# A two-block network on one core: output products of two heads issued together in the second attention, S5 tables computed beside the experts, four norms whose roots use 128 columns, and a row maximum taken in the instruction that adds the bias

## The reference, cut to what matters

```
def first_block(x, c, ...):
    for layer in range(DEPTH):                      # DEPTH = 2
        h = modulate(rmsnorm(x, norm1_w[layer]), shift1, scale1)
        if layer % 2 == 0:
            ...  mix = concat([pool_mixer(u), chunk_attention(q, k, v, rel_bias)]) @ mix_w_out
        else:
            mix = mamba2_mixer(h, ...)
        x = x + gate1 * mix
        h2 = modulate(rmsnorm(x, norm2_w[layer]), shift2, scale2)
        x = x + gate2 * hier_moe(h2, ...)           # 32 experts, top 2 per token
    return rmsnorm(x, final_norm_w)
...
def fox_attention(q, k, v, f_logit, q_gain, k_gain):  # 8 heads of 64, 512 rows
    q, k = rms_norm(q, q_gain), rms_norm(k, k_gain)
    c = cumsum(log_sigmoid(f_logit))
    s = (q @ k.T) * B_HEAD_DIM ** -0.5 + c[query] - c[key]
    s = where(key <= query, s, NEG_INF)
    return softmax(s) @ v
...
def s5_mixer(u, a_re, a_im, log_dt, b_re, b_im, c_re, c_im, d):  # 64 groups, 64 states, 16 channels
    dt = exp(log_dt)
    ab = exp(a * dt)                                # complex, from magnitude, sine and cosine
    bb = (ab - 1) / a * b                           # complex, 64 x 64 x 16
    x_t = ab * x_(t-1) + bb @ u_t                   # scan over 512 rows
    return real(c @ x) + d * u
...
def second_block(x, p, ...):
    for i in range(DEPTH):
        h = rms_norm(x, norm_mix[i])
        if i % 2 == 0:  x = x + concat([gmlp_mixer(u_a, v_a), fox_attention(...)]) @ ev_w_out
        else:           x = x + glu(gelu(s5_mixer(h)))
        x = x + conv_ffn(rms_norm(x, norm_ffn[i]))
        x = x + sigmoid(rms_norm(x) @ ple_w_gate) * (p[i] @ ple_w_proj)
```

## Time and profile before

| | |
|---|---|
| median of 3 runs | 2632.39 us (2631.26 to 2634.85) |
| the profiled execution | 2631.74 us |
| its span in the trace | 2630.0 us |
| mean granted clock of PE | 0.944 of full speed |
| busy share | PE 90%, PEld 69%, DVE 59%, POOL 56%, ACT 27% |
| moved by DMA | 374.40 MB, mean 142 GB/s |

### The profile page before, as it was taken

One profiled execution on the slowest core, in us unless ns is written; L12 is line 12 of the kernel. 1 busy time (PEld: TensorE's weight loads), 2 busy tenths in 40 slices (PEclk: granted clock), 3 DMA queues, 4 the chain that ended last, 5 costly groups with the idle time before them and its releaser, 6 DMA issues.

```text
span 2630.0 us, 33090 instructions
## 1 busy us (share of the span) xinstructions
PE 2366.2 (90%) x12200; PEld 1806.6 (69%) x12200; DVE 1558.4 (59%) x1986; ACT 700.7 (27%) x1170; POOL 1484.7 (56%) x1272
## 2 busy tenths in 40 slices
PE   4988989959999998896798799999987899999998
PEld 2764755537777776553585588888866788888887
DVE  6879832166878765224897666662249926666223
ACT  2113212223434422122223232220025613222011
POOL 4830345455554552553672166667779657666774
PEclk7977989979999997998897999999998999999999
DMA  8845879533323234994331133332330223333231
GB/s 318 255 162 206 293 285 360 190 125 105 102 91 112 93 112 178 393 357 163 84 116 60 49 96 96 96 96 93 114 97 25 57 64 96 96 96 96 88 112 64
DMA packets 316737, 374.40 MB, mean 142 GB/s; under 512 B 52250, under 2 KB 259886, under 8 KB 316502
## 3 DMA queue, kind: packets, MB, share of 16 engines
q1 hardware_dynamic: 253840, 313.82, 35.6%
q0 software_dynamic: 28352, 31.04, 3.6%
q10 hardware_dynamic: 34438, 28.08, 3.5%
HBM read 410.20 MB, written 39.68 MB: 171 GB/s over the span
## 4 chain that ended last, share of the span: by engine, by line
PE 29%; issue 24%; POOL 23%; DVE 11%; DMA 10%; ACT 1%; POOLq 0%; ACTq 0%; SPq 0%; DVEq 0%
POOL WL L853 15%; PE PAIR L545 6%; POOL WH L849 6%; PE PAIR L546 6%; PE PAIR L547 6%; DMA XG<-htok_scratch,GATHER_I 4%; PE BANK L1823 4%; DMA ADA_A<-in_ada_w 2%; PE BANK L2259 1%; PE PAIR L1847 1%; PE PAIR L1809 1%; DVE ADA_SUM L652 1%; DMA PAIR_W<-y_scratch 1%; POOL EXTRA_W L2007 1%; DMA RAW<-in_ffn_w_up 1%
## 5 line engine op out<-in xcount | busy, mean ns | idle before, releaser
L853 POOL TENSOR_TENSOR WL<-RAW,WH 128x512 fp32r<-128x512 f32 x584 | 819.0, 1432 | 12.2
L545 PE MATMUL PAIR<-HH,WH 128*128 128x512 f32 x1792 | 710.0, 396 | 39.4 <-POOL HL L1142 27.2
L546 PE MATMUL PAIR<-HL,WH 128*128 128x512 f32 x1792 | 700.9, 391 | 0.0
L547 PE MATMUL PAIR<-HH,WL 128*128 128x512 f32 x1792 | 700.7, 391 | 0.0
L848 POOL TENSOR_TENSOR TURN<-ONES 128x1 f32<-128x1 f32 x146 | 36.8, 252 | 848.7 <-PE PAIR L547 751.3
L545 PEld LDWEIGHTS PAIR<-HH,WH 128*128 128x128 f32 x1792 | 338.6, 189 | 123.2 <-issue 44.2
L546 PEld LDWEIGHTS PAIR<-HL,WH 128*128 128x128 f32 x1792 | 338.9, 189 | 71.0 <-issue 2.2
L547 PEld LDWEIGHTS PAIR<-HH,WL 128*128 128x128 f32 x1792 | 338.4, 189 | 71.5
L849 POOL TENSOR_SCALAR WH<-RAW 128x2048 fp32r<-128x2048 f32 x146 | 284.7, 1950 | 0.0
L545 PE MATMUL PAIR<-FHH,WH 128*128 128x512 f32 x352 | 138.7, 394 | 0.0
L547 PE MATMUL PAIR<-FHH,WL 128*128 128x512 f32 x352 | 138.0, 392 | 0.0
(11 more groups left out here) (540 smaller groups left out, 4074.7 us busy)
## 6 DMA issues: line engine op xcount, KB each, us to landing
PAIR_W<-in_moe_w SPq DMA_DIRECT2D x96, 1024.0 KB, 9.9
RAW<-in_ffn_w_up SPq DMA_DIRECT2D x88, 512.0 KB, 4.8
ADA_B<-in_ada_w SPq DMA_DIRECT2D x30, 1024.0 KB, 5.3
RAW<-in_ssm_w_in SPq DMA_DIRECT2D x48, 512.0 KB, 4.8
ADA_A<-in_ada_w SPq DMA_DIRECT2D x18, 1024.0 KB, 6.9
RAW<-in_ffn_w_down SPq DMA_DIRECT2D x32, 512.0 KB, 4.2
RAW<-in_ev_w_in SPq DMA_DIRECT2D x20, 512.0 KB, 4.6
RAW<-in_mix_w_in SPq DMA_DIRECT2D x16, 512.0 KB, 6.6
```

Of the source, the lines that this page charges most:

```text
L545: nc.tensor.matmul(o, wh, xh, start=start, stop=False)
L546: nc.tensor.matmul(o, wh, xl, start=False, stop=False)
L547: return nc.tensor.matmul(o, wl, xh, start=False, stop=stop)
L853: ins = pool.tensor_tensor(WL[:, s, c], RAW[:, s, c], WH[:, s, c].bitcast(F32), ALU.subtract)
```

## The change

The diff does five things.

1. **Norms 0, 2, 8 and the final one.** The sums are formed by four products per tile with 32 columns of ones each, so that row block j of 128 stands in partitions 32j to 32j + 31 and only 128 columns are left. Root and reciprocal work on 128 columns. Four products with one column of the identity spread the factor over 128 partitions and 512 columns of a PSUM bank, and DVE multiplies X by that bank. The final norm's weighted sum is made by PE too.
2. **S5 tables.** The vectors, powers, B products, angles and TURN_NEW are computed in MoE 1: DVE does one slice after HID of slots 1 to 10 and 12 to 19, ACT one in slots 0, 2, 8, 11 and 13 to 20. BRAW is loaded in slot 0, and the TURN_NEW saves go out on ACT's queue, not SP's. TAB stays in SBUF, so its save and reload are gone.
3. **Maximum.** In both attentions one instruction adds the bias and takes the row maximum. The factor HD ** -0.5 goes into the copy of Q (att0) or the gain of Q (att1).
4. **Outputs in att1.** The products of two heads are issued after the odd head's transposes and scores, alternating between the two halves of 64 columns.
5. `dve_sum` of the final norm is gone from the residual's loop, and `pool_s5_index` moves ahead into MoE 1.

```diff
+    def pe_sums(bank, at, weights, tile, first, last):
+        for j in range(NT):
+            ins = nc.tensor.matmul(bank[32 * j:32 * j + 32, at:at + P], weights, tile[:, j * P:j * P + P], start=first, stop=last)
+        return ins
...
-            ins = nc.tensor.matmul(bank[:], ONES[:], SQ[:, k % 2, :], start=k == 0, stop=k == KD - 1)
+            ins = pe_sums(bank, 0, ONES[:, 0:32], SQ[:, k % 2, :], k == 0, k == KD - 1)
...
+    def pe_factor(b, at):
+        for j in range(NT):
+            ins = nc.tensor.matmul(BANK[b % 4][:, j * P:j * P + P], IDENT[:, 32 * j:32 * j + 1].broadcast_to([P, P]),
+                                   RSTD[:, at:at + P], start=True, stop=True)
+        ins.then_inc(bank_ready, 1)
...
+        both, one = (take_bank(pe, plan.b[f"norm{FINAL}"] + i) for i in range(2))
+        for k in range(KD):
+            pe.wait(sq_ready)
+            weighted = pe_sums(both, 0, FINAL_SQ[:, k:k + 1].broadcast_to([P, 32]), SQ[:, k % 2, :], k == 0, k == KD - 1)
+            ins = pe_sums(one, 0, ONES[:, 0:32], SQ[:, k % 2, :], k == 0, k == KD - 1)
...
-            if k >= 2:
-                act.wait(part_used)
-            act.e.activation(TMP[:, k % 2, :], X[:, k, :], ACT.Square, scale=norm_gain[FINAL](k)).then_inc(part_ready, 1)
-        act.passed(part_used, 1)
...
-        dve.e.scalar_tensor_tensor(RSTD[:], FINAL_VAR, EPS, RSTD[:], ALU.mult, ALU.add).then_inc(var_ready, 1)
+        both, one = RSTD[:, 0:P], RSTD[:, P:2 * P]
+        dve.link(dve.e.tensor_scalar(both, full_bank(dve, b)[:, 0:P], 1.0 / D, None, ALU.mult))
+        c = b + 1
+        dve.e.tensor_scalar(one, full_bank(dve, c)[:, 0:P], 1.0 / D, EPS, ALU.mult, ALU.add).then_inc(bank_free[c % 4], 1)
+        dve.e.wait_ge(bank_free[c % 4], c // 4 + 1)
+        dve.e.scalar_tensor_tensor(both, one, EPS, both, ALU.mult, ALU.add).then_inc(var_ready, 1)
         dve.wait(root_ready)
-        dve.e.reciprocal(RSTD[:], RSTD[:]).then_inc(bank_free[b % 4], 1)
-        dve.e.wait_ge(bank_free[b % 4], b // 4 + 1)
+        dve.e.reciprocal(both, both).then_inc(bank_free[b % 4], 1)
+        dve.e.reciprocal(one, one).then_inc(total_ready, 1)
...
-            dve.e.scalar_tensor_tensor(norm_buffer(k), X[:, k, :], BOTH_GAIN[:, k:k + 1], RSTD[:], ALU.mult, ALU.mult).then_inc(norm_pre, 1)
+            dve.e.scalar_tensor_tensor(norm_buffer(k), X[:, k, :], BOTH_GAIN[:, k:k + 1], factor[:], ALU.mult, ALU.mult)\
+                 .then_inc(norm_pre if k < KD - 1 else bank_free[b % 4], 1)
...
-                ins = dve.e.scalar_tensor_tensor(HF[:, k, :], X[:, k, :], gain(k), RSTD[:], ALU.mult, ALU.mult)
-                if k in (0, KD - 1):
+                ins = dve.e.scalar_tensor_tensor(HF[:, k, :], X[:, k, :], gain(k), factor[:], ALU.mult, ALU.mult)
...
-        act_copy_pairs(act, "mixin", 2, 2, Q0, False)
+        act_copy_pairs(act, "mixin", 2, 2, Q0, False, scale=HD ** -0.5)
...
+        def outputs(heads):
+            p = p0 + 1
+            pe.e.wait_ge(evac[p % 2], p // 2 + max(0, heads[0] // 2 * 2 - 2))
+            for h in heads:
+                b = att_bank(n, h, 3)
+                pe.e.wait_ge(bank_free[b % 4], b // 4 + 1)
+            o = out_half(n, heads[0] // 2)
             for kt in range(NT):
-                ins = nc.tensor.matmul(o[a:a + HD, kt * P:SEQ], v[:, kt, h * HD:h * HD + HD],
-                                       pt[:, h % 2, TRI_AT[kt]:TRI_AT[kt] + SEQ - kt * P],
-                                       start=kt == 0, stop=kt == NT - 1)
-            ins.then_inc(w["out"], 1)
+                for h in heads:
+                    a = (h % 2) * HD
+                    ins = nc.tensor.matmul(o[a:a + HD, kt * P:SEQ], v[:, kt, h * HD:h * HD + HD],
+                                           pt[:, h % 2, TRI_AT[kt]:TRI_AT[kt] + SEQ - kt * P],
+                                           start=kt == 0, stop=kt == NT - 1)
+            ins.then_inc(w["out"], len(heads))
...
-            outputs(h)
+            if n == 0:
+                outputs((h,))
+            elif h % 2:
+                outputs((h - 1, h))
...
-                    ins = dve.e.scalar_tensor_tensor(s[:, h % 2, SEG[j]:SEG[j] + wide], bank[:, at:at + wide],
-                                                     HD ** -0.5, bias(h)[:, SEQ - wide:SEQ], ALU.mult, ALU.add)
+                    ins = dve.e.tensor_tensor_reduce(s[:, h % 2, SEG[j]:SEG[j] + wide], bank[:, at:at + wide],
+                                                     bias(h)[:, SEQ - wide:SEQ], 1.0, LOWEST, ALU.add, ALU.max,
+                                                     MX[:, h % 2, 0, j:j + 1])
...
-            for j in range(NT):
-                ins = dve.e.tensor_reduce(MX[:, h % 2, 0, j:j + 1], s[:, h % 2, SEG[j]:SEG[j] + P * (j + 1)], AX.X, ALU.max)
-            dve.link(ins)
...
-            elif h:
-                dve_s5_turning(dve, h - 1)
...
-        if n:
-            dve_s5_turning(dve, KD - 1)
...
+                if layer:
+                    act_s5_slice(act, s)
...
+            if layer:
+                dve_s5_slice(dve, s)
...
+            dve_final_gains(dve)
+            for par in range(2):
+                dve.e.wait_ge(turn_saved[par], 8 * KD)
...
-            if layer and i:
-                for k in (2 * i - 2, 2 * i - 1):
-                    dve_sum(dve, k, TMP)
-        if layer:
-            for k in (KD - 2, KD - 1):
-                dve_sum(dve, k, TMP)
...
-    def sp_s5_reload(engine):
-        w, sp = s5_sems, engine.e
-        engine.wait(w["spilled"], 32)
-        engine.wait(half_ready, 4)
-        sp.dma_start(TAB[:].rearrange("p a t n -> p (a t n)"), tab_dram).then_inc(w["tab_back"], 16)
-    def sp_s5_save(engine):
-        w, sp = s5_sems, engine.e
-        for k in range(KD):
-            par = k % 2
-            engine.wait(w["turning"], 2)
-            sp.dma_start(turn_dram[k], TURN_NEW[:, par].rearrange("p a t n -> p (a t n)")).then_inc(turn_saved[par], 16)
...
+    def act_s5_load_b(act):
+        act.e.wait_ge(moe_sems["saved"], 2 * 16 * NT)
+        for i, name in enumerate(("od_b_re_2", "od_b_im_2")):
+            act.e.dma_start(BRAW[:, i], t[name][0].rearrange("(t h) p c -> (h p) t c", h=2)).then_inc(s5_sems["b_landed"], 16)
...
+    def act_s5_slice(act, s):
+        if s == 0:
+            act_s5_exp(act)
+            act_s5_load_b(act)
+        if s == 2:
+            act_s5_vectors(act)
+        if s == 8:
+            act_s5_save_b(act)
+        if s == 11:
+            act_s5_tables(act)
+        if 13 <= s < 13 + KD:
+            act_s5_save_turning(act, s - 13)
...
+    def dve_s5_slice(dve, s):
+        if s == 1:
+            dve_s5_angles(dve)
+        if s == 2:
+            dve_s5_series(dve)
+        if s == 3:
+            dve_s5_first_power(dve)
+        if s == 4:
+            dve_s5_ratios(dve)
+        if s == 5:
+            dve_s5_powers(dve)
+        if s == 6:
+            dve_s5_step(dve)
+        if s == 7:
+            dve_s5_b(dve)
+        if s in (8, 9, 10):
+            dve_s5_turns(dve, s - 8)
+        if 12 <= s < 12 + KD:
+            dve_s5_turning(dve, s - 12)
```

More of the change, by code:

```diff
@@ L27 @@
 NEG = -1e30
+LOWEST = -3e38
 UNIT = 2048
@@ L87, in norm @@
     def norm(n):
-        plan.step(f"norm{n}", banks=0 if n in (1, 3) else 1)
+        plan.step(f"norm{n}", banks={1: 0, 3: 0, 2: 2, 4: 4, 5: 0, 8: 2}.get(n, 1))
     def moe(layer):
         plan.step(f"moe{layer}", pairs=NT + 2 * PAIRS + 4, banks=5)
+        if layer:
+            plan.step("s5a", banks=1)
         plan.step(f"slots{layer}", banks=2 * PAIRS)
@@ L118, in make_plan @@
     moe(1)
-    plan.step("s5a", banks=1)
     norm(4)
@@ L1149, in dve_rstd, with dve_root @@
         dve.link(dve.e.reciprocal(tile, tile))
-    def dve_root(dve, n):
+    def dve_root(dve, n, columns=SEQ):
         b = plan.b[f"norm{n}"]
-        bank = full_bank(dve, b)
-        dve.e.tensor_scalar(RSTD[:], bank[:], 1.0 / D, EPS, ALU.mult, ALU.add).then_inc(var_ready, 1)
+        bank, tile = full_bank(dve, b), RSTD[:, 0:columns]
+        dve.e.tensor_scalar(tile, bank[:, 0:columns], 1.0 / D, EPS, ALU.mult, ALU.add).then_inc(var_ready, 1)
         dve.wait(root_ready)
-        dve.e.reciprocal(RSTD[:], RSTD[:]).then_inc(bank_free[b % 4], 1)
+        dve.e.reciprocal(tile, tile).then_inc(bank_free[b % 4], 1)
         dve.e.wait_ge(bank_free[b % 4], b // 4 + 1)
@@ L1220, in pe_mixin, with act_copy_pairs @@
             pe_ada(pe, q)
-    def act_copy_pairs(act, name, first, n, to, tokens, func=ACT.Copy):
+    def act_copy_pairs(act, name, first, n, to, tokens, func=ACT.Copy, scale=1.0):
         for i in range(n):
@@ L3016, in sp_s5_tables @@
         if first == 0:
+            engine.wait(w["spilled"], 16)
+            for par in range(2):
+                engine.wait(turn_saved[par], 8 * KD)
             sp.dma_start(BB[:].rearrange("p a t c -> p (a t c)"), bb_dram).then_inc(w["reloaded"], 16)
@@ L3126, in dve_s5_vectors, with dve_s5_ratios @@
```

(7 more changed lines are left out.)

253 lines of the change are left out of this document (137 added, 116 removed).

## The result

The changed kernel takes 2613.0 us (2611.9 to 2614.1, 4 runs) against 2633.3 us of the kernel before: ratio 0.9923, 95% interval 0.9906 to 0.9941. It is faster by 20 us, where 41 were forecast. The profiled execution has a span of 2612.3 us at a mean clock of 0.936. Times were measured on several chips, on which the kernel before took 2633 to 2638 us, so kernels are compared by their ratio to it, or stage by stage in their traces.

The account below looks back on a forecast made before the run. PE bounds the long products, so gains come only where it waits; DVE sets the pace in att1. Terms -28 - 5 - 9.5 - 2.3 - 4 - 0.5 + 8 = -41.3 from 2632.4 give 2591 us, range 2575 to 2615.

Parts of the forecast that it names:

- The pair of heads in att1: Att1: a pair takes 10.8 us at full clock plus 1.5 for copies, 12.3; the stage gains 28 us.
- The clock in att1: Att1: PE's clock is low only in the first pair, rising some 11 us after the restart.
- rival 1: Att1: PE's clock stays low, so the stage gains 5 to 12 us instead of 28; 2610 us; chance 0.15.
- MoE 1: MoE 1: added DMA bytes and ACT's BRAW issue and table loads cost +8 us (0 to +18).
- Its ACT term: MoE 1: HT waits behind ACT's BRAW issue in slot 0, with table loads in four slots: 3 us.
- The slower rival: MoE 1 slot 0: BRAW's issue lasts ten times as long or more, PE stands still; about 2645 us; chance 0.05.
- The bytes' term: MoE 1: 5.2 MB of added transfers is 16 us at 317 GB/s, of which about a half shows.
- Fused maximum: Both attentions: fused instructions cost 1.68 us for four, reads 0.1 to 0.19 each; price per head falls by about 1.2.
- The rival with the scan's price: Attentions: the fused instruction costs like the scan, att0 gains nothing, att1 loses 4 of 28; 2600 us; chance 0.10.
- the reading that carries over a sentence of the Trainium skill: Attentions: halved two-source throughput applied regardless of PSUM, so the fused group costs 3.4 us and nothing is won.
- Final norm and norm 2: Final norm: earlier X and shorter reciprocal, -9.5 us (-6 to -11); norm 2: shorter reciprocal and neighbours, -2.3 us.
- Norm 8: Norm 8: cheaper products from PSUM and shorter reciprocal, which the stage mostly keeps, -4 us (-2 to -5.5).

Follow-up runs that it names:

- the second profile: The changed kernel itself, unedited, run and profiled again on another occasion; 2612.6 us, ratio 0.9907 to the kernel before.
- experiment 1: Changed kernel, but in att1 DVE divides head h + 1 before it adds the bias for head h + 2; 2601.5 us, ratio 0.9859.
- experiment 2: Changed kernel with each att1 head's outputs behind its own scores again; 2599.4 us, ratio 0.9855.
- experiment 3: Changed kernel with two unused products of 512 columns behind each even head's scores in att1; 2597.4 us, ratio 0.9843.
- Experiment 8: Changed kernel with att1's division moved early, BRAW on SyncE's queue, and five unused products before att1's first transposes; 2584.0 us, ratio 0.9789.
- experiment 4: Changed kernel with BRAW's two loads on SyncE's queue before its first slot wait in MoE 1, not ACT's in slot 0; 2601.4 us, ratio 0.9871.
- experiment 11: Experiment 8's kernel, but both attentions add and take the maximum in two instructions again; 2598.0 us, ratio 0.9859.
- the mended kernel: The kernel of Experiment 8: changed kernel with early division, BRAW on SyncE's queue and five unused products in att1; 2584.0 us.

## Why the prediction was wrong

The total was -20.3 us where -41.3 was forecast. It lies inside the stated range, 2575 to 2615, near its end. Step by step:

- **The pair of heads in att1 failed.** The text said: a pair is 10.8 us at full clock "and I add 1.5 for the copies of the odd head". The outputs in turn do cost 2.37 for sixteen records, as forecast, and the first transposes come 10.4 us after the first scores (10.6 said; 12.9 in the second profile). But the wait that they uncover was not seen. DVE's order is division (h), addition (h + 2), division (h + 1), so transposes (h + 1) of an odd head came 2.2 us after scores (h + 2) each time. Experiments 1, 2 and 3 remove or fill this one wait and gain 9 to 11 us each. From the first transposes on, the pairs took 22.1, 19.0, 18.3 and 6.8 us, where 17.0, 12.3, 12.3 and 7.3 were said.
- **The clock in att1 failed, as rival 1.** "As before, some 11 us after the restart", then full speed to the end. The low clock came back with each wait of 2.2 us, so it was low for most of the stage (0.70). Experiment 8 shows the price of the start alone: 7.3 us. The rival had 0.15, a gain of 5 to 12 in att1 (measured 11.6 and 8.2) and a time of 2610, which is near the result. Its reason, waits on ACT, was not the one found: PE waited for DVE. It should have had more, since the trace of before already had the clock at 1.2 GHz after such a wait:

```profile
1435.12 1.94 PE L1373 MATMUL PAIR<-IDENT,S 128*128 128x128 f32 x8 [2.42 <-issue]
```

The longer wait of 3.08 us in the earlier trace rows left the clock at full speed, so that trace did not settle it.
- **MoE 1 was mis-sized: +8, measured +15.9 and +14.7.** Its ACT term was 3 us, though the BRAW issue of 5.14 and a table load already exceed that; PE's wait for the copy behind the issue was 10.1 us, and experiment 4 takes 10 to 11 us off the stage. The 5.14 us of the earlier trace rows was taken over from a place before which the DMA engines were nearly idle (share 0.02 from 1265 to 1277). The slower rival named this very mechanism with tenfold lengths. It was real with 2.7 times the length. The bytes' term, half of 16, was of the right size: leaving out 3.8 of the 5.2 MB gives 3 to 7.
- **Fused maximum: right.** 0.69 for 512 columns and 0.08 a read. The rival with the scan's price falls. So does the reading that carries over a sentence of the Trainium skill (Vector Engine (DVE) Microarchitecture Reference, Points that are easy to get wrong) to one source in PSUM. What the sentence itself says, of two sources in SBUF, no run here shows. Its worth in the whole kernel was set too low, at -5 in att0 and 2.7 at the start of att1; experiment 11 shows 14 us in the mended kernel, through later waits and the clock.
- **Final norm and norm 2: right.** -10.9 (-9.5 said), -2.7 and -1.9 (-2.3 said). **Norm 0** gave -2.0 for -0.5.
- **Norm 8: right in its prices, wrong in what the stage keeps.** "What it gains the stage mostly keeps" was said of DVE, with -4. The products cost 0.67 each, as forecast, and the first scan came 4.7 us nearer, but the stage gave only 1.1 and 0.6, since DVE then waited for products that wait for ACT. The table's -3.8 and -3.4 beside -4 is luck: 2.7 of it is the output product behind att1 that starts at full clock, which the prediction put at nothing. No run tested the reason for the loss.
- **Evin: right within what profiles differ by.** It takes 130.1 to 132.9 us in all thirteen profiles, the kernel before among the longer ones.
- **Overlap of the two column halves: right.** Sixteen records of outputs in 2.37 us, as eight had the earlier trace rows. The rule of the Trainium skill (TensorEngine Tiling (Array Packing), Theoretical Speedup), up to twice for a dimension of 64, agrees with the trace. What it is worth in the kernel is another matter, 2.3 us and not 9.

The change as a whole: the norms give about 16 us (10.9, 2.7, 1.1 and 2.0 in the first profile), the fused maximum and the turning's leaving give what att0 and att1 gained, and MoE 1 takes 15 back. The pairing of outputs costs 9 us as it stands (experiment 2). That the norms' part is theirs was read from the traces; no run undid them alone, and none kept the turning in att1 alone.

## What to carry to other kernels

Before moving work off a place in an engine's order, ask which wait it covers there. A product that seems to cost 2.4 us costs next to nothing if the engine would wait 2.2 us in its stead, and where the clock falls with such waits, as in the changed kernel, it even pays. In a loop over several engines look at each in-order queue for an instruction that is ready but stands behind one that waits; exchanging the two was worth more here than halving the products. And do not take over the issue time of a transfer of many small pieces from another place: the same one held its queue for 2.5, 5.1 or 13.9 us here, while the DMA engines moved 96, 154 or over 320 GB/s.
